# The last norm of a fused decoder layer, shared among three engines

## The chip, the cores and the metric

One Trainium2 chip, one core in use. The metric is the device time of one execution in microseconds (us). Engines: TensorE (PE in the profile), VectorE (DVE), ScalarE (ACT), GpSimd (POOL) and SyncE (SP), which here only starts DMA transfers. All data is float32; fp32r is the same 32 bits, written in the form that the matmuls read.

## The reference

One layer of a decoder on 544 tokens (512 of a prompt, 32 of 8 samples with 4 tokens each), 1024 channels. It has a joint input projection, dilated attention in three groups, a convolution branch, a merge with a norm, and then a mixture of 32 experts, of which each token uses two. What the change touches is the last step:

```python
def layer_norm(x, g, b):
    xf = x.astype(jnp.float32)
    mu = jnp.mean(xf, -1, keepdims=True)
    var = jnp.mean(jnp.square(xf - mu), -1, keepdims=True)
    return ((xf - mu) * lax.rsqrt(var + LN_EPS) * g.astype(jnp.float32) + b.astype(jnp.float32)).astype(x.dtype)

return layer_norm(DN_ALPHA * h + hierarchical_moe(h, ...), ln2_g, ln2_b)
```

`ln2_g` and `ln2_b` are vectors of 1024, one value for each channel.

## The kernel before, in words

The program is one launch with a written-out instruction list for each engine; semaphores order them. Its stages follow one another: projection (until about 165 us on GpSimd's side, with TensorE, ScalarE and VectorE), gates with attention and convolution (until about 420), merge of the two branches and first norm (L1424 to L1481), routing, and the 32 experts (from about 590 to 1143 us). There each weight matrix is split in two parts, the high one cast by ScalarE (L1153), the low one subtracted by VectorE (L1607), and multiplied on TensorE. GpSimd gathers the rows of an expert and scatters the results with an indirect DMA that adds in DRAM, into the buffer `expert_rows` (`y_dram`), which already holds the residual h. The experts' results come scaled by 1/alpha, so the buffer holds (alpha h + moe)/alpha, and the last norm uses EPS / ALPHA**2.

The tail begins when the last scatter has landed. GpSimd then raises `over_done` (L1823). SyncE, which waited for it (L524), loads the 544 rows in five tiles with five DMAs (L527), 128 rows of 1024 in each of the first four and 32 rows in the last (`TILES`, `NTT` = 5). The tiles `fh[0..3]` lie in `region_b`, `fh[4]` in `region_a`. `g2row` and `b2row` are `ln2_g` and `ln2_b`, broadcast to 128 partitions; they were loaded long before (L506, L507, semaphore `rows2_loaded`).

VectorE takes one tile after another (L1685 to L1692): `statistics` (L1441 to L1447: two `bn_stats` of 512 columns, `bn_aggr`, and an addition of eps) raises `hvar`; then it subtracts the mean and multiplies by `g2row` in one 1024-column `scalar_tensor_tensor` (L1689); waits for ScalarE's square root (L1245 to L1247, semaphore `hsd`); takes the reciprocal (L1691); and multiplies by it and adds `b2row` in a second 1024-column `scalar_tensor_tensor` (L1692), which raises `fdone`. The helper `link` makes VectorE wait for the completion of its own instruction before the next that reads its result. SyncE waits for `fdone` tile by tile and stores each tile to the output (L529 to L531). The small columns (`stats`, `mv`, `var_e`, `sd`, `rs`, `nmr`) exist twice and alternate from tile to tile.

ScalarE and GpSimd have nothing else to do in the tail: ScalarE takes the five roots, and after `over_done` GpSimd only waits for copies and stores that ended long before. Other lines that the rows name: L1294 is the convolution on VectorE (a `scalar_tensor_tensor` with two SBUF tensors, 128x512 and 128x32), L1710 GpSimd's part in splitting the projection's weights, L1739 GpSimd's sum of the two branches, beside which VectorE runs L1422 and L1435 (subtractions of SBUF tensors), L1428 and L1429 (one operand in PSUM). L1033, L1077 and L1082 are ScalarE's Identity of the gates, Sqrt and Silu of the convolution branch, and L1184 its scaling of an expert's result from PSUM.

Of the kernel before, what the change touches and what calls it, by code (L numbers as in the profile page):

```python
# [21 lines left out]
ACT = mybir.ActivationFunctionType  # L22
# [19 lines left out]
ALPHA = 2 ** 0.25  # L42
EPS = 1e-5
# [13 lines left out]
TILES = [(t * P, min(P, N - t * P)) for t in range((N + P - 1) // P)]  # L57
NTT = len(TILES)
# [51 lines left out]
def build(nc, a, o):  # L110
# [14 lines left out]
    with ExitStack() as ctx:  # L125
# [3 lines left out]
        def sem(name):  # L129
            return ctx.enter_context(nc.semaphore(name))  # L130
# [95 lines left out]
        def ln_cols(first, width=1):  # L226
            return [small[:, 18 * q + first:18 * q + first + width] for q in range(2)]

        stats, mv, var_e, sd, rs, nmr = ln_cols(0, 12), ln_cols(12, 2), ln_cols(14), ln_cols(15), ln_cols(16), ln_cols(17)
# [48 lines left out]
        def places(a_, b_):  # L278
# [56 lines left out]
        y_ps, y_used, hvar, hsd, hdone = (  # L335
            sem(x) for x in ("y_ps", "y_used", "hvar", "hsd", "hdone"))
# [14 lines left out]
        over_done = sem("over_done")  # L351
        fin_loaded = [sem(f"fin_loaded{t}") for t in range(NTT)]
        rows2_loaded = sem("rows2_loaded")
        fdone = sem("fdone")
        xg_zero, y_stored = sem("xg_zero"), sem("y_stored")
        qbd_zero, br_loaded = sem("qbd_zero"), sem("br_loaded")

# [2 lines left out]
        fh = [raw[0][:, t * D:(t + 1) * D] for t in range(4)] + [raw[2][:, 0:D]]  # L360
        g2row, b2row = raw[2][:, D:2 * D], raw[2][:, 2 * D:3 * D]
# [26 lines left out]
        def _(sp_e):  # L388
# [79 lines left out]
            for t in range(NTT):  # L468
                c0, n = TILES[t]
# [56 lines left out]
            for t, (c0, n) in enumerate(TILES):  # L526
                sp_e.dma_start(fh[t][0:n], y_dram[c0:c0 + n]).then_inc(fin_loaded[t], 16)  # L527
            for t, (c0, n) in enumerate(TILES):
                sp_e.wait_ge(fdone, t + 1)  # L529
                dst = y_p[:, t, :] if t < 4 else y_sample.rearrange("b t d -> (b t) d")  # L530
                sp_e.dma_start(dst, fh[t][0:n]).then_inc(y_stored, 16)  # L531
            sp_e.wait_ge(y_stored, 16 * NTT)
# [3 lines left out]
        def _(pe):  # L536
# [55 lines left out]
            def conv_rows(_):  # L592

                pe.wait_ge(u_set, 1)
                pe.wait_ge(state_sb, 1)
                for c in range(CT):
                    pe.transpose(ps[0:PAD, 6, c * P:(c + 1) * P], uext[:, c, SEQ:SEQ + PAD], eye)
                for c in range(CT):
                    last = pe.transpose(ps[0:NS, 7, c * P:(c + 1) * P], cst_u[:, c, :], eye)
                last.then_inc(u_ps, 1)  # L600
# [23 lines left out]
            def sample_rows(_):  # L624

                pe.wait_ge(v_sb, 6)
                for m in range(12):
                    last = pe.transpose(ps[0:NS, 2 + m // 4, (m % 4) * P:(m % 4) * P + P], zqkv[:, K0 + m, SEQ:N], eye)
                last.then_inc(s_ps, 1)
# [33 lines left out]
            def new_keys(_):  # L663
                pe.wait_ge(k_sb, 6)
                for m in range(6):
                    last = pe.matmul(ps[0:NS, 6, m * 64:(m + 1) * 64], zqkv[:, K0 + m, SEQ:N],
                                     qbd[:, m, :, :].rearrange("p b j -> p (b j)"), start=True, stop=True)
                last.then_inc(st_ps, 1)
# [315 lines left out]
        def _(ac):  # L984
# [251 lines left out]
            with ac.If(count > 0):  # L1236
                with ac.Fori(0, count) as i:
                    for f in range(KF):
# [3 lines left out]
                    ac.activation(yo[0].rearrange("p (h n) -> p h n", h=2), ps[0:BLK, 6:8, :], ACT.Identity,  # L1242
                                  scale=rowgate[:, bass.ds(i + NE, 1)]).then_inc(yo_sb, 1)

            for t, (c0, n) in enumerate(TILES):  # L1245
                ac.wait_ge(hvar, NTT + t + 1)
                ac.activation(sd[t % 2][0:n], var_e[t % 2][0:n], ACT.Sqrt).then_inc(hsd, 1)  # L1247


        @block.vector  # L1250
        def _(ve):
            chain = [0]

            def link(ins):

                chain[0] += 1
                ins.then_inc(dve_chain, 1)
                ve.wait_ge(dve_chain, chain[0])
# [165 lines left out]
            for m in range(KD):  # L1424
                s = 4 * (m % 2)
# [15 lines left out]
            def statistics(rows, s, n, done, eps):  # L1441

                for half in range(2):
                    st = ve.bn_stats(stats[s][0:n, 6 * half:6 * half + 6], rows[:, half * 512:(half + 1) * 512])
                link(st)
                link(ve.bn_aggr(mv[s][0:n], stats[s][0:n, :]))
                ve.tensor_scalar(var_e[s][0:n], mv[s][0:n, 1:2], eps, None, ALU.add).then_inc(done, 1)  # L1447
# [13 lines left out]
            for t, (c0, n) in enumerate(TILES):  # L1461
                s = t % 2
# [5 lines left out]
                hs = hrow[0:n, s, :]  # L1468
# [213 lines left out]


            ve.wait_ge(rows2_loaded, 32)
            for t, (c0, n) in enumerate(TILES):  # L1685
                s, hs = t % 2, fh[t][0:n]
                ve.wait_ge(fin_loaded[t], 16)
                statistics(hs, s, n, hvar, EPS / ALPHA ** 2)
                link(ve.scalar_tensor_tensor(hs, hs, mv[s][0:n, 0:1], g2row[0:n], ALU.subtract, ALU.mult))  # L1689
                ve.wait_ge(hsd, NTT + t + 1)  # L1690
                link(ve.reciprocal(rs[s][0:n], sd[s][0:n]))  # L1691
                ve.scalar_tensor_tensor(hs, hs, rs[s][0:n], b2row[0:n], ALU.mult, ALU.add).then_inc(fdone, 1)  # L1692


        @block.gpsimd
        def _(po):
# [118 lines left out]
            with po.If(count > 0):  # L1815
                with po.Fori(0, count) as i:
# [4 lines left out]
                    po.wait_ge(scattered[0], 16 * i + 16 * (NE // 2 + 1))  # L1821
                    po.sem_inc(pool_steps, 1)
            po.nop().then_inc(over_done, 1)  # L1823

            po.wait_ge(copied, 16 * 4 * NB)
            po.wait_ge(stored, 16 * STORES)
# [48 lines left out]
```

## Time and profile before

| | us |
|---|---|
| median of 3 runs (lowest to highest) | 1179.59 (1179.41 to 1184.06) |
| the profiled execution, its own time | 1181.13 |
| its span in the trace | 1179.10 |
| last norm, first statistics to end of span | 24.05 |

The span is what the trace covers; the execution's own time has 2.03 us more around it. Times in the trace count from the start of the span. PE is busy for 1102.8 us, DVE 820.6, ACT 582.3, POOL 268.2. A line of a group of instructions gives line, engine, operation, tile names, shapes, count, then busy time in all and the mean of one in ns, then idle time before them.

### The profile page before, as it was taken

To read this page: it belongs to the slowest core of one execution; us is meant where nothing else is said; L and a number is where in the kernel's file an instruction comes from. 1 tells how busy PE (TensorE), PEld (TensorE's weight loads), DVE (VectorE), ACT (ScalarE), POOL (GpSimd) and SP (SyncE) were. 2 spreads that over 40 slices of the span, in tenths; PEclk is the share of its full clock that TensorE was granted. 3 is DMA by queue.
4 is the path that set the end of the run, shared out by engine and by line. 5 is a ranking of instruction groups with operands and counts; after the bars stand their busy time and mean duration, and the time that the engine had idled before them with its cause. 6 is when DMAs were issued, how large, how long until landed. Compare 5 with 4: busy or idle time off the path is not lost.

```text
span 1179.1 us, 16033 instructions
## 1 busy us (share of the span) xinstructions
PE 1102.8 (94%) x5990; PEld 879.5 (75%) x5990; DVE 820.6 (70%) x929; ACT 582.3 (49%) x524; POOL 268.2 (23%) x185
## 2 busy tenths in 40 slices
PE   6999999999999999994999999999999999999970
PEld 5999998789888888763677777777777777777750
DVE  1079999810116728526699998888888888988857
ACT  2232221011115661003568777787787787787740
POOL 2344440000000015001022332322313313323100
PEclk9999999999999999986899999999999999999995
DMA  6476723136422540317699999999999999999813
GB/s 246 150 272 244 303 109 152 63 121 192 154 90 97 226 148 1 112 72 310 223 353 369 368 371 360 362 360 357 360 357 357 366 360 352 368 357 368 314 48 151
DMA packets 40336, 293.06 MB, mean 249 GB/s; under 512 B 10927, under 2 KB 14639, under 8 KB 24557
## 3 DMA queue, kind: packets, MB, share of 16 engines
q1 hardware_dynamic: 26029, 262.53, 58.9%
q0 software_dynamic: 10720, 25.98, 7.6%
q10 hardware_dynamic: 3552, 4.06, 1.0%
q8 instruction: 25, 0.41, 0.1%
q14 instruction: 10, 0.08, 0.0%
HBM read 286.83 MB, written 41.12 MB: 278 GB/s over the span
## 4 chain that ended last, share of the span: by engine, by line
PE 89%; DVE 4%; DMA 2%; POOL 2%; ACT 1%; issue 1%; POOLq 0%; SPq 0%; ACTq 0%; DVEq 0%
PE ps L587 10%; PE ps L902 10%; PE ps L904 10%; PE ps L903 10%; PE ps L926 5%; PE ps L928 5%; PE ps L927 5%; PE ps L549 3%; PE ps L551 3%; PE ps L550 3%; PE ps L805 3%; PE ps L885 2%; PE ps L770 2%; PE ps L659 2%; PE ps L833 2%; PE ps L835 2%
## 5 line engine op out<-in xcount | busy, mean ns | idle before, releaser
L1607 DVE TENSOR_TENSOR region_b_split<-region_b,z_split 128x2048 fp32r<-128x2048 f32 x96 | 216.9, 2286 | 26.0 <-ACT z_split L1153 25.5
L1607 DVE TENSOR_TENSOR region_a_split<-region_a,z_split 128x2048 fp32r<-128x2048 f32 x96 | 216.7, 2286 | 23.1 <-ACT z_split L1153 23.0
L902 PE MATMUL ps<-z_split,scratch_split 128*96 128x512 f32 x512 | 206.8, 404 | 1.9 <-DVE scratch_split L1612 1.9
L904 PE MATMUL ps<-z_split,scratch_split 128*96 128x512 f32 x512 | 202.1, 395 | 0.0
L1153 ACT CAST z_split<-region_a 128x2048 fp32r<-128x2048 f32 x96 | 179.8, 1908 | 0.0
L1153 ACT CAST z_split<-region_b 128x2048 fp32r<-128x2048 f32 x94 | 176.2, 1908 | 2.0 <-PE ps L904 2.0
L1294 DVE SCALAR_TENSOR_TENSOR z_conv_gates<-scratch,column_vectors,z_conv_gates 128x512 f32<-128x512 f32 (+1 forms) x240 | 133.9, 640 | 0.0
L587 PE MATMUL ps<-x_columns,region_b 128*128 128x272 f32 x512 | 127.1, 396 | 0.0
L549 PE MATMUL ps<-z_split,region_b_split 128*128 128x272 f32 x384 | 111.1, 289 | 3.5 <-POOL region_b_split L1710 3.5
L551 PE MATMUL ps<-z_split,region_b_split 128*128 128x272 f32 x384 | 111.2, 290 | 0.0
L904 PEld LDWEIGHTS ps<-z_split,scratch_split 128*96 128x96 f32 x512 | 83.2, 163 | 36.7
L902 PEld LDWEIGHTS ps<-z_split,scratch_split 128*96 128x96 f32 x512 | 85.3, 167 | 33.8 <-DVE scratch_split L1612 2.2
L550 PE MATMUL ps<-z_split,region_b_split 128*128 128x272 f32 x384 | 110.4, 288 | 0.0
L587 PEld LDWEIGHTS ps<-x_columns,region_b 128*128 128x128 f32 x512 | 94.4, 190 | 17.3
L926 PE MATMUL ps<-z_split,x_columns_split 128*96 128x512 f32 x256 | 101.1, 395 | 2.0 <-issue 1.2
L903 PE MATMUL ps<-region_b_split,scratch_split 128*96 128x512 f32 x256 | 101.5, 396 | 0.0
L928 PE MATMUL ps<-z_split,x_columns_split 128*96 128x512 f32 x256 | 100.9, 394 | 0.0
L903 PE MATMUL ps<-region_a_split,scratch_split 128*96 128x512 f32 x256 | 100.5, 393 | 0.0
L1710 POOL TENSOR_TENSOR region_b_split<-region_b,region_b_split 128x1024 fp32r<-128x1024 f32 x24 | 67.0, 2810 | 83.5 <-ACT region_b_split L1009 83.5
L1033 ACT ACTIVATE z_conv_gates<-ps,column_vectors 128x272 f32<-128x272 f32 x32 | 15.6, 487 | 124.7 <-PE ps L587 124.5
L549 PEld LDWEIGHTS ps<-z_split,region_b_split 128*128 128x128 f32 x384 | 72.3, 188 | 4.3 <-issue 3.0
L1771 POOL DMA_INDIRECT expert_rows<-value_rows,block_rows x26 | 67.6, 2600 | 23.2 <-POOL block_rows L1768 23.2
(262 smaller groups left out, 1757.4 us busy)
## 6 DMA issues: line engine op xcount, KB each, us to landing
region_b<-in_w_expert_gate SPq DMA_DIRECT2D x16, 2048.0 KB, 11.7
region_a<-in_w_expert_up SPq DMA_DIRECT2D x16, 2048.0 KB, 11.8
region_a<-in_w_expert_gate SPq DMA_DIRECT2D x16, 2048.0 KB, 11.7
region_a<-in_w_expert_down SPq DMA_DIRECT2D x16, 2048.0 KB, 11.4
region_b<-in_w_expert_up SPq DMA_DIRECT2D x16, 2048.0 KB, 12.2
region_b<-in_w_expert_down SPq DMA_DIRECT2D x16, 2048.0 KB, 11.4
region_b<-in_w_in_pairs SPq DMA_DIRECT2D x21, 1024.0 KB, 4.8
region_b<-in_cache_tiles POOLq DMA_DIRECT2D x16, 768.0 KB, 4.9
```

The source lines that it names most:

```text
L549: pe.matmul(out, w_hi[:, s, k, tile], x_hi[:, k, cols], start=k == 0, stop=False)
L550: pe.matmul(out, w_hi[:, s, k, tile], x_lo[:, k, cols], start=False, stop=False)
L551: last = pe.matmul(out, w_lo[:, s, k, tile], x_hi[:, k, cols], start=False, stop=k == KD - 1)
L587: last = pe.matmul(ps[:, half, 0:HALF], wring[:, j % 2, k, (t % 2) * P:(t % 2 + 1) * P], xt[:, k, half * HALF:(half + 1) * HALF], start=k ...
L902: pe.matmul(out, xh[:, k, :], hi[:, k, :], start=k == 0, stop=False)
L903: pe.matmul(out, xh[:, k, :], lo[:, k, :], start=False, stop=False)
L904: last = pe.matmul(out, xl[:, k, :], hi[:, k, :], start=False, stop=k == KD - 1)
L926: pe.matmul(out, hh[:, k, :], hi[:, k, cols], start=k == 0, stop=False)
L928: last = pe.matmul(out, hl[:, k, :], hi[:, k, cols], start=False, stop=k == KF - 1)
L1153: ac.copy(high_part[w][:, part], raw[place][:, part]).then_inc(high_set[w], 1)
L1294: ve.scalar_tensor_tensor(dst, win(k), wdw_c[:, bass.ds(k * CT + c, 1)], dst, ALU.mult, ALU.add).then_inc(conv_step, 1)
L1607: ve.tensor_tensor(low_part[place][:, part], raw[place][:, part], high_part[high or w][:, part].bitcast(F32), ALU.subtract).then_inc(low_s ...
```

## The change

For the four full tiles the norm is written as x * r + (-mean * r), then times `ln2_g`, then plus `ln2_b`, where r is the reciprocal root. ScalarE does the first (one `Identity` with scale and bias for each partition), VectorE the multiplication, GpSimd the addition. VectorE also computes -mean * r (`nmr`). VectorE takes the statistics of tile t+1 before the reciprocal of tile t, and multiplies tile t-1 after that. The fifth tile (32 rows) keeps the old form and comes last, with its statistics moved up.

```diff
@@ sync
             for t, (c0, n) in enumerate(TILES):
-                sp_e.wait_ge(fdone, t + 1)
+                if t < NTT - 1:
+                    sp_e.wait_ge(fdone, t + 1)
+                else:
+                    sp_e.wait_ge(fdone_last, 1)
@@ scalar
-            for t, (c0, n) in enumerate(TILES):
+            def last_root(t):
+                n = TILES[t][1]
                 ac.wait_ge(hvar, NTT + t + 1)
                 ac.activation(sd[t % 2][0:n], var_e[t % 2][0:n], ACT.Sqrt).then_inc(hsd, 1)
+
+
+            last_root(0)
+            for t in range(NTT - 1):
+                last_root(t + 1)
+                ac.wait_ge(frs, t + 1)
+                ac.activation(fh[t], fh[t], ACT.Identity, scale=rs[t % 2], bias=nmr[t % 2]).then_inc(fscaled, 1)
@@ vector
-            for t, (c0, n) in enumerate(TILES):
-                s, hs = t % 2, fh[t][0:n]
+            def last_statistics(t):
+                n = TILES[t][1]
                 ve.wait_ge(fin_loaded[t], 16)
-                statistics(hs, s, n, hvar, EPS / ALPHA ** 2)
-                link(ve.scalar_tensor_tensor(hs, hs, mv[s][0:n, 0:1], g2row[0:n], ALU.subtract, ALU.mult))
+                statistics(fh[t][0:n], t % 2, n, hvar, EPS / ALPHA ** 2)
+
+            def last_scale(t):
+                s = t % 2
                 ve.wait_ge(hsd, NTT + t + 1)
-                link(ve.reciprocal(rs[s][0:n], sd[s][0:n]))
-                ve.scalar_tensor_tensor(hs, hs, rs[s][0:n], b2row[0:n], ALU.mult, ALU.add).then_inc(fdone, 1)
+                link(ve.reciprocal(rs[s], sd[s]))
+                ve.scalar_tensor_tensor(nmr[s], mv[s][:, 0:1], -1.0, rs[s], ALU.mult, ALU.mult).then_inc(frs, 1)
+
+            def last_multiply(t):
+                ve.wait_ge(fscaled, t + 1)
+                ve.tensor_tensor(fh[t], fh[t], g2row, ALU.mult).then_inc(fmul, 1)
+
+            full = NTT - 1
+            last_statistics(0)
+            for t in range(full):
+                last_statistics(t + 1)
+                last_scale(t)
+                if t >= 1:
+                    last_multiply(t - 1)
+            last_multiply(full - 1)
+            t, n = full, TILES[full][1]
+            s, hs = t % 2, fh[t][0:n]
+            link(ve.scalar_tensor_tensor(hs, hs, mv[s][0:n, 0:1], g2row[0:n], ALU.subtract, ALU.mult))
+            ve.wait_ge(hsd, NTT + t + 1)
+            link(ve.reciprocal(rs[s][0:n], sd[s][0:n]))
+            ve.scalar_tensor_tensor(hs, hs, rs[s][0:n], b2row[0:n], ALU.mult, ALU.add).then_inc(fdone_last, 1)
@@ gpsimd, after over_done
+            po.wait_ge(rows2_loaded, 32)
+            for t in range(NTT - 1):
+                po.wait_ge(fmul, t + 1)
+                po.tensor_tensor(fh[t], fh[t], b2row, ALU.add).then_inc(fdone, 1)
```

## Rows read from the trace of the kernel before

**Rows 1.** The page: the chain that ended last, share of the span by engine.
```profile
PE 89%; DVE 4%; DMA 2%; POOL 2%; ACT 1%; issue 1%; POOLq 0%; SPq 0%; ACTq 0%; DVEq 0%
```

**Rows 2.** Busy time of each engine in the tail (x instructions), clock, DMA.
```profile
core 0: us, PE busy (x) PEld busy (x) DVE busy (x) ACT busy (x) POOL busy (x), PEclk, DMA share, GB/s
...
1155.05:1176.80 21.75, 0.00 (x0) 0.00 (x0) 21.02 (x35) 1.01 (x5) 0.00 (x0) 0.50 0.39 158
```

**Rows 3.** Timeline of tile 0 in the tail: start, duration, engine, line.
```profile
1155.05 1.28 DVE L1444 BATCH_NORM_STATS2 small<-region_b 128x6 f32<-128x512 f32 x2 [9.73 <-DMA region_b<-expert_rows]
...
1156.69 1.28 DVE L1689 SCALAR_TENSOR_TENSOR region_b<-region_b,small,region_a 128x1024 f32<-128x1024 f32 x1
1158.00 0.16 DVE L1691 RECIPROCAL small<-small 128x1 f32<-128x1 f32 x1
1158.20 1.28 DVE L1692 SCALAR_TENSOR_TENSOR region_b<-region_b,small,region_a 128x1024 f32<-128x1024 f32 x1
```

**Rows 4.** DMA issues of the tail: timeline, and median time to landing (last number).
```profile
1151.31 0.33 SPq L527 DMA_DIRECT2D region_b<-expert_rows  x1
...
region_b<-expert_rows SPq DMA_DIRECT2D x1, 512.0 KB, 3.6
...
1151.69 0.90 SPq L527 DMA_DIRECT2D region_b<-expert_rows  x2
...
region_b<-expert_rows SPq DMA_DIRECT2D x2, 512.0 KB, 4.1
...
1153.11 0.68 SPq L527 DMA_DIRECT2D region_a<-expert_rows  x1
...
region_a<-expert_rows SPq DMA_DIRECT2D x1, 128.0 KB, 6.4
...
out<-region_b SPq DMA_DIRECT2D x4, 512.0 KB, 2.6
out<-region_a SPq DMA_DIRECT2D x1, 128.0 KB, 1.9
```

**Rows 5.** Groups by form, with means; then L1710 and L1739, shortest/median/longest ns.
```profile
L1307 DVE TENSOR_TENSOR region_a<-region_a,value_rows 128x544 f32<-128x544 f32 x12 | 8.7, 725 | 0.4
...
L1607 DVE TENSOR_TENSOR region_b_split<-region_b,z_split 128x2048 fp32r<-128x2048 f32 x96 | 216.9, 2286 | 26.0 <-ACT z_split L1153 25.5 <-POOLq L1777 0.4
...
L1563 DVE SCALAR_TENSOR_TENSOR w_attn<-w_attn 128x10 f32<-128x10 f32 x4 | 0.7, 170 | 0.1
...
L1184 ACT ACTIVATE value_rows<-ps,row_gates 96x1024 f32<-96x1024 f32 x32 | 35.5, 1111 | 8.2 <-PE ps L928 8.2
...
L1710 POOL TENSOR_TENSOR region_b_split<-region_b,region_b_split x24: 2344/2393/4987, 16.5 to 164.2; 128x1024 fp32r<-128x1024 f32 x24
...
L1739 POOL TENSOR_TENSOR z_conv_gates<-z_conv_gates x8: 1344/2540/3317, 425.2 to 463.7; 128x544 f32<-128x544 f32 x8
```

**Rows 6.** Timeline of ScalarE around the Sqrt of the convolution branch.
```profile
355.59 0.61 ACT L1077 ACTIVATE ps<-ps 128x544 f32<-128x544 f32 x1
...
360.14 0.49 ACT L1033 ACTIVATE z_conv_gates<-ps,column_vectors 128x272 f32<-128x272 f32 x1 [3.94 <-PE ps L587]
360.64 1.28 ACT L1082 ACT_TABLE_LOAD   x1
```

**Rows 7.** Timelines of VectorE and GpSimd where they meet.
```profile
440.92 0.71 DVE L1429 TENSOR_TENSOR z_conv_gates<-ps,z_conv_gates 128x544 f32<-128x544 f32 x1
441.55 2.28 DVE L1435 TENSOR_TENSOR region_b_split<-region_b,region_a_split 128x2048 fp32r<-128x2048 f32 x1
443.75 1.86 DVE L1422 TENSOR_TENSOR z_split<-z_conv_gates,z_split 128x544 fp32r<-128x544 f32 x1
...
441.72 3.32 POOL L1739 TENSOR_TENSOR z_conv_gates<-z_conv_gates 128x544 f32<-128x544 f32 x1 [3.75 <-DVE z_conv_gates L1429]
...
86.24 2.42 DVE L1294 SCALAR_TENSOR_TENSOR z_conv_gates<-scratch,column_vectors,z_conv_gates 128x32 f32<-128x32 f32 x1
...
86.07 2.54 POOL L1710 TENSOR_TENSOR region_b_split<-region_b,region_b_split 128x1024 fp32r<-128x1024 f32 x1 [6.08 <-ACT region_b_split L1009]
```

More of the change, by code:

```diff
@@ L353, in build @@
         rows2_loaded = sem("rows2_loaded")
-        fdone = sem("fdone")
+        fdone, fdone_last, frs, fscaled, fmul = (sem(x) for x in ("fdone", "fdone_last", "frs", "fscaled", "fmul"))
         xg_zero, y_stored = sem("xg_zero"), sem("y_stored")
```

## The prediction, made before the changed kernel was built or timed

> **What bounds the kernel now.** I read the page first. The chain that ended last is 89% PE [rows 1], so over the whole kernel the matrix engine is the bound; the change touches only what comes after it, and the next view is the busy time by stretch from the moment the last norm begins. There PE, PEld and POOL have no work, DVE is busy 21.02 of the 21.75 us of the five tiles and ACT 1.01 [rows 2]. VectorE is therefore the bound of the tail: a fifth of that for each tile, a little over 4.3 us. The timeline of one tile [rows 3] gives the steps: 1.64 us from the first statistics instruction to the subtract-and-multiply (L1689), 1.28 for that, 0.16 for the reciprocal (0.20 to the next start), 1.28 for the multiply-and-add (L1692). These four follow each other without a gap, so ACT's square root (1.01 for five, 0.20 each [rows 2]) is hidden behind L1689. The loads of the tiles [rows 4] land at 1154.9 (1151.31 + 3.6) for tile 0 and at 1159.5 (1153.11 + 6.4) for tile 4; only the first is waited for. Tile 1, issued at 1151.69, takes about 4.6 (the mean of it and tile 0 is 4.1) and lands at 1156.3. The last store is issued at the end of the stretch of rows 2 and lands 1.9 later [rows 4]; the span, 1179.1, ends 0.4 after that. From the start of statistics of tile 0 (1155.05, which I call 0 from here) the end is thus at 24.05, made of 21.7 of VectorE and 2.3 of store and end.
>
> **The change, part by part.** Up to 0 nothing moves. In the four full tiles VectorE loses both 1024-column operations, 2 x 1.28, and gets one 1024-column tensor_tensor and one 128x1 scalar_tensor_tensor. Between 544 columns (725 ns) and 2048 columns (2286 ns) [rows 5] a tensor_tensor takes 1.04 ns a column, so 1024 columns take 725 + 480 x 1.04 = 1.22 us. The 128x1 one is near the 128x10 one, 0.17 us. A full tile costs VectorE 1.64 + 0.20 + 0.17 + 1.15 to 1.22, about 3.2 instead of 4.33. That saves 4.5 us of VectorE over four tiles, if nothing stops it.
>
> ScalarE gets a 1024-column Identity a tile. The nearest row is L1184, an Identity with a scale over 96x1024, 1.11 us [rows 5]; I take 1.10, and 1.3 would change nothing but the start of m3 below. With the root it is 1.3 us a tile, beside VectorE's 3.2, so it hides; if that cover went, only the one of tile 3 would be on the path, 1.1 us. Does Identity after Sqrt load a table? No: after the Sqrt of L1077 at 355.59, an Identity of L1033 ran at 360.14 with no load of its own; the next load (1.28) belongs to the Silu of L1082 [rows 6]. I cost table loads at nothing, and at 2 x 1.28 a tile if this were wrong.
>
> GpSimd gets four additions of 128x1024 f32. It did the same size and kind (a subtraction, L1710) in 2.34 at least and 2.39 in the median, and 128x544 in 1.34 at least [rows 5]. I take 2.39. But both rows have maxima, 4.99 and 3.32, and rows 7 show where they come from. At 441.72 GpSimd's 544-column addition meets VectorE's 2048-column subtraction (441.55, 2.28 long): it takes 3.32, so it ends 1.2 after VectorE's. VectorE's next, 544 columns, starts at 443.75 and takes 1.86 in place of 0.72: it ends 0.57 after GpSimd's. At 86.24 a VectorE scalar_tensor_tensor of only 32 columns takes 2.42, and ends 0.05 after GpSimd's 1024-column operation (86.07 + 2.54). So two operations that each read two SBUF tensors do not overlap at all; one waits the whole length of the other, and each turn under a wait gives back about 0.13 (3.32 - 2.11 = 1.21 against 1.34 own time; 0.57 against 0.72). In the new tail these are the addition, the multiply, the 128x1 scalar_tensor_tensor (two tensor inputs, however small) and both 1024-column operations of tile 4.
>
> The Trainium skill (SBUF — State Buffer, section "SBUF: two separate sides") calls this an exclusive lock and extends it to VectorE operations with one input where they run in a two-port mode. No row shows that beside a GpSimd addition; by it the 128x1 additions of the statistics would wait as well, the VectorE steps behind them would slip by about 0.35 in two tiles, and the sum would come to +1.5 instead of the value below.
>
> Now the order, with s statistics, r reciprocal, n the 128x1 operation, m multiply, a addition (times from 0):
> - s0 0, s1 1.64 (landed at 1.3), r0 3.28, n0 3.48, s2 3.65 (tiles 1 and 4 land at 1.3 and 4.5, tile 2 a third of the way, about 2.4), r1 5.29, n1 5.49, m0 5.66 to 6.88. ScalarE scaled tile 0 from 3.7 to 4.8, so m0 waits for nothing.
> - a0 6.97 to 9.36 (L1429 ends at 441.63 and the addition that waits for it starts at 441.72 [rows 7], so a hand-over is 0.09). Beside it s3 6.80 to 8.44 and r2; n2 at 8.64 is held until 9.4. m1 to 10.6.
> - a1 10.65 to 13.04, beside it s4 and r3; n3 at 12.35 is held to 13.07. m2 to 14.2.
> - ScalarE scales tile 3 only after n3, 13.13 to 14.23. m3 asks at 14.27, a2 at 14.29. From here on VectorE's two-input work and GpSimd's form one queue: m3 1.22, a2 2.39, first operation of tile 4 1.28, a3 2.39, second operation of tile 4 1.28.
> With a turn each: m3 to 15.5, a2 to 17.75, tile 4's first to 18.9, a3 to 21.1, tile 4's second to 22.3. Then 1.9 for the small store and 0.4 for the end: 24.6, which is 0.55 later than 24.05. Other turns are possible, since GpSimd's longest L1710 took 4.99 against 2.39 [rows 5], more than any single VectorE operation beside it there would make it wait, so it must have lost more than one turn. a2, a3, then tile 4: 25.0. Both of tile 4 ahead of a3: a3 ends at 22.3 to 22.5, its 512 KB store takes 2.6 [rows 4] and the small one follows it, 25.4. So +0.5 to +1.4; I take +0.8.
>
> Other edits cost nothing I can find: SP's extra semaphore only names the last wait; its order of stores is the same, and tile 4's is behind tile 3's, as above. GpSimd's additions stand behind over_done, which SP needs, but are only reached after it, and nothing behind them but the waits at the end of the program. Each store is issued later than now for tile 0 (9.4 in place of 4.4), and hides.
>
> The profiled execution was 1181.13 with a span of 1179.1; the median of the runs is 1179.59. The difference of +0.8 makes a span of 1179.9, and on the median 1180.4.
>
> **Rivals.**
> - *The two engines overlap after all.* Then a0 to 9.36, m1 8.8 to 10.0, a1 to 12.5, m2 to 13.2, a2 to 15.7, a3 to 18.05; VectorE is through at 16.9. Store of tile 3 to 20.7, of tile 4 to 21.1, end 21.5: -2.6, 1177.0. For it: these lines are not the same pair (additions in f32 and a multiply, where rows 7 have fp32r results and a subtraction). Against it: three pairs of shapes in two stages show whole waits.
> - *All of VectorE stands still under an addition, the statistics too.* This one ends slower. Then nothing overlaps after m0: VectorE's 5 x 1.64 + 4 x 0.37 + 4 x 1.2 + 2.7 = 17.2 and GpSimd's 9.56 give 26.8, less 0.8 for turns, and 2.3 for store and end: 28.3, +4.2, 1183.8. Place: s3, s4 and the reciprocals beside a0 and a1. It decides over my case as soon as a pair of batch_norm_stats (1.28 us [rows 3]) stretches beside an addition. Nothing shows a one-input operation beside one of GpSimd's additions; every wait that rows 7 show is of an operation with two tensor inputs, so I hold it unlikely. For a slowdown over 0.5% (5.9 us) each addition would have to be dearer than 2.39 by 0.4 us besides, or by 1.3 without this.
> - *Identity does reload the table*, so that ScalarE needs 3.9 a tile. It would be later than VectorE in tile 3 by up to 2.6: 1183.0. Rows 6 speak against it.
>
> **How the numbers follow.** The forecast (alternating turns) 0.82, overlap 0.07, all held 0.08, table loads 0.03. My case with its bounds is 1180.1 to 1181.0. The wider lock of the Trainium skill's SBUF page would give 1181.1. The runs before spread from 1179.41 to 1184.06 with two of three within 0.2. The range goes 2 below, towards overlap without reaching it, and 3 above to 1183.4, which takes in the table loads and an addition dearer by 0.5 each. A measurement of this kernel can tell about 0.5%, 5.9 us, from no change. Faster by that would need more than the whole saving of VectorE (4.5): 0.02. Slower by it needs the dearer additions just priced: 0.05. The rest, 0.93, is within it.
>
> **What would show it.** In the changed profile: POOL with four additions, 2.3 to 2.5 us where not waiting, longer late in the tail; multiplies of 1.2 us, at least one of 2 us or more; the 128x1 operation mean well over 0.17 us (two of four held by 0.7); a pair of batch_norm_stats still 1.28; one ACT table load in the tail; last store issued near 22.3 after the first statistics. I am wrong if the multiplies and additions lie beside each other at their own lengths, or if the statistics stretch.

## The result, and the profile after

The changed kernel takes 1189.11 us in the median of 14 runs (1183.97 to 1191.44); the kernel before, in the same number of runs, 1182.35 (1179.00 to 1186.38). The ratio is 1.0051, with a 95% interval of 1.0033 to 1.0068: slower by 6.0 us, with 3.9 and 8.0 as ends. A second measurement (below) gave 1.0044 (1.0021 to 1.0067). The forecast was +0.8 us with a range up to 1183.4; the kernel is slower than that.

The profiled execution of the changed kernel has a time of 1188.84 and a span of 1186.5. It splits at the first statistics of the last norm. Before, that was at 1155.05 with 24.05 behind it [rows 2]; now it is at 1158.14 with 28.36 behind it. So 3.1 us of the difference of these two executions lie ahead of anything that the change touches, and 4.3 in the tail. Another 0.3 lie outside the span: an execution's own time has 2.3 us more than its span here (2.0 before), and the same 0.3 shows in all 25 runs of the changed kernel against the 28 of the second measurement's kernel before; no run explains it. First the tail, in the timeline (start, duration, engine, line; idle time and releaser in brackets), from tile 2's statistics on:

```profile
1164.69 1.28 DVE L1455 BATCH_NORM_STATS2 small<-region_b 128x6 f32<-128x512 f32 x2
1164.93 2.34 POOL L1859 TENSOR_TENSOR region_b<-region_b,region_a 128x1024 f32<-128x1024 f32 x1 [15.39 <-DVE region_b L1709]
...
1166.51 0.77 DVE L1705 SCALAR_TENSOR_TENSOR small<-small 128x1 f32<-128x1 f32 x1
1167.20 1.21 DVE L1709 TENSOR_TENSOR region_b<-region_b,region_a 128x1024 f32<-128x1024 f32 x1
...
1172.06 2.34 POOL L1859 TENSOR_TENSOR region_b<-region_b,region_a 128x1024 f32<-128x1024 f32 x1 [1.23 <-DVE region_b L1709]
1172.15 3.33 DVE L1709 TENSOR_TENSOR region_b<-region_b,region_a 128x1024 f32<-128x1024 f32 x1 [0.17 <-ACT region_b L1258]
1175.40 1.27 DVE L1721 SCALAR_TENSOR_TENSOR region_a<-region_a,small 32x1024 f32<-32x1024 f32 x1
1175.56 3.31 POOL L1859 TENSOR_TENSOR region_b<-region_b,region_a 128x1024 f32<-128x1024 f32 x1 [1.16 <-DVE region_b L1709]
1176.70 0.15 DVE L1723 RECIPROCAL small<-small 32x1 f32<-32x1 f32 x1
1176.89 3.06 DVE L1724 SCALAR_TENSOR_TENSOR region_a<-region_a,small 32x1024 f32<-32x1024 f32 x1
...
1178.89 0.33 SPq L534 DMA_DIRECT2D out<-region_b  x1
1179.97 0.33 SPq L534 DMA_DIRECT2D out<-region_a  x1
```

These answer to [rows 3] and [rows 7]. VectorE and GpSimd take turns as forecast: the statistics (1.28, not stretched) lie beside an addition, while the 128x1 operation (0.77 instead of 0.16), the multiply of tile 3 (3.33 instead of 1.22) and the last operation (3.06 instead of 1.27) stand still under one. The last store starts at 1179.97, 21.83 after the first statistics. Before it was 21.74. Up to here the tail has lost 0.1 us.

But the span goes on to 1186.5. Before, 2.3 us followed the last store; now 6.5 do, and in them no engine is busy:

```profile
core 0: us, PE busy (x) PEld busy (x) DVE busy (x) ACT busy (x) POOL busy (x), PEclk, DMA share, GB/s
1158.14:1179.97 21.83, 0.00 (x0) 0.00 (x0) 21.08 (x35) 5.97 (x9) 10.32 (x4) 0.50 0.35 140
1179.97:1186.50 6.53, 0.00 (x0) 0.00 (x0) 0.00 (x0) 0.00 (x0) 0.00 (x0) 0.50 0.24 83
```

The instructions at the end of the program are not counted as busy and stand in no group. The view of one source line shows them: L125 is the `with` statement at whose exit each engine's list closes. Its columns are shortest/median/longest ns and the start. First the changed kernel, then the kernel before:

```profile
L125 PEldq DRAIN  x1: 752/752/752, 1147.3 to 1147.3; - x1
L125 ACTq DRAIN  x1: 1271/1271/1271, 1170.9 to 1170.9; - x1
...
L125 POOLq DRAIN  x1: 10503/10503/10503, 1175.8 to 1175.8; - x1
L125 DVEq DRAIN  x1: 3097/3097/3097, 1176.9 to 1176.9; - x1
...
L125 SPq DRAIN  x1: 13/13/13, 1182.2 to 1182.2; - x1
```

```profile
L125 POOLq DRAIN  x1: 7420/7420/7420, 1151.7 to 1151.7; - x1
...
L125 SPq DRAIN  x1: 13/13/13, 1178.9 to 1178.9; - x1
```

Each engine ends with a DRAIN, and then all of them meet. GpSimd's took 7.42 us before, from 1151.7 to 1159.1, while VectorE was at the end of the first tile, which it left at 1159.4: hidden by 19.8 us. Now it is issued at 1175.8, waits for the last addition (1175.56 + 3.31 = 1178.87), and ends at 1186.3, 7.43 after that. SyncE, which had seen all stores land at 1182.2, waited 4.1 us for GpSimd.

### The profile page after: what moved, and what is told of

It reads as the page before. It is cut to its first block, busy times and chain, and to the rows that moved or that the text cites. A ratio compares the mean times of both kernels' runs of the same rounds, so it can differ in the third digit from the quotient of the medians.

```text
span 1186.5 us, 16038 instructions
## 1 busy us (share of the span) xinstructions
PE 1106.3 (93%) x5990; PEld 883.6 (74%) x5990; DVE 820.6 (69%) x929; ACT 587.2 (49%) x528; POOL 278.6 (23%) x189
## 4 chain that ended last, share of the span: by engine, by line
PE 89%; DVE 4%; DMA 2%; POOL 2%; issue 1%; ACT 1%; POOLq 0%; SPq 0%; ACTq 0%; DVEq 0%
PE ps L590 10%; PE ps L905 10%; PE ps L907 10%; PE ps L906 10%; PE ps L929 5%; PE ps L931 5%; PE ps L930 5%; PE ps L552 3%; PE ps L554 3%; PE ps L553 3%; PE ps L808 2%; PE ps L888 2%; PE ps L773 2%; PE ps L662 2%; PE ps L836 2%; PE ps L837 2%
## 5 line engine op out<-in xcount | busy, mean ns | idle before, releaser
L590 PE MATMUL ps<-x_columns,region_b 128*128 128x272 f32 x512 | 130.5, 404 | 0.0
L1803 POOL DMA_INDIRECT expert_rows<-value_rows,block_rows x26 | 67.6, 2601 | 23.2 <-POOL block_rows L1800 23.2
```

Of the source, the lines that this page charges most:

```text
L590: last = pe.matmul(ps[:, half, 0:HALF], wring[:, j % 2, k, (t % 2) * P:(t % 2 + 1) * P], xt[:, k, half * HALF:(half + 1) * HALF], start=k ...
```

## The experiments

Nine of the twelve are single executions with a profile; three were also timed. I count the tail from the first statistics of the last norm to the end of the span, and give times in it from that point, as in the prediction. No matmul runs in it: two profiles of the changed kernel gave 28.36 and 28.45, and three kernels whose tail is that of before 24.05, 24.1 and 24.1, so one profile tells 0.1 us.

### Is it DRAIN, and what does it depend on?

The kernel before, with GpSimd made to wait for the last tile:

```diff
+            po.wait_ge(fdone, NTT)
             po.wait_ge(copied, 16 * 4 * NB)
```

> The kernel before with one wait more: at the end of its instruction list GpSimd waits for the last tile (fdone = 5) and does nothing in the tail. I count the tail from the first statistics of the last norm to the end of the span: 24.05 us before, 28.36 after the change. Theory A (GpSimd's DRAIN at the end of the program takes 7.4 us from GpSimd's last instruction, and the end of the program waits for it; it has nothing to do with the additions): the tail is 21.74 + 0.1 + 7.42 + 0.2 = 29.4 us, DRAIN stays 7.42. Theory C (the long end comes from the additions themselves): the tail stays at 24.1.

Measured: tail 29.5 us (1155.16 to 1184.7), DRAIN 7.42. A kernel with no addition on GpSimd loses 5.5 us by where its DRAIN lies. Theory C falls. DRAIN does not wait for a transfer of GpSimd either: it was issued at 1177.1, 22 us after the first tile of the tail, which is loaded only when the last scatter has landed, and it took the same 7.42.

With an early DRAIN besides:

```diff
             po.nop().then_inc(over_done, 1)
+            po.drain()
...
+            po.wait_ge(fdone, NTT)
```

> As the run before, with a DRAIN of GpSimd more, right behind over_done, that is over long before the end. Theory A (7.4 us whenever it runs): first and last DRAIN both 7.4, tail 29.4 us. Theory B (DRAIN works off what GpSimd's indirect DMAs of the experts have left, so the first one pays and a second is short, as the 0.18 us one at the start of the program): last DRAIN near 0.2, tail 24.1 us.

```profile
L1824 POOLq DRAIN  x1: 7420/7420/7420, 1156.8 to 1156.8; - x1
...
L125 POOLq DRAIN  x1: 40/40/40, 1182.4 to 1182.4; - x1
```

The early one (L1824) took 7.42 and the last one 0.04; the tail is 24.1 us. Theory A falls too: DRAIN has no fixed price, it works off something that an earlier DRAIN can work off.

The same line in the changed kernel:

> The changed kernel with a DRAIN of GpSimd right behind over_done, 10 us before its first addition. Theory A: tail 28.4 us as in the changed kernel. Theory B: last DRAIN short, the end is set by the last store, 21.83 + 2.1 + 0.4 = 24.3 us.

```profile
L1856 POOLq DRAIN  x1: 7420/7420/7420, 1157.0 to 1157.0; - x1
...
L125 POOLq DRAIN  x1: 3135/3135/3135, 1178.4 to 1178.4; - x1
```

Tail 24.7 us (1160.72 to 1185.4), in place of 28.4. The last DRAIN is issued beside the last addition and ends 0.1 us behind it, so additions add nothing to it. Theory B held, with a miss of 0.4: it gave 24.3. SyncE had seen the stores land at 24.1, as in the changed kernel, and the last 0.4 lie between two semaphore instructions of GpSimd (1184.9 and 1185.3); the same 0.4 is there in a second profile of this kernel, and no run explains it.

Three tiles shared, the addition of tile 3 on VectorE (SyncE's waits and GpSimd's loop, changed to match, are not shown):

```diff
-                ve.tensor_tensor(fh[t], fh[t], g2row, ALU.mult).then_inc(fmul, 1)
+                if t < 3:
+                    ve.tensor_tensor(fh[t], fh[t], g2row, ALU.mult).then_inc(fmul, 1)
+                else:
+                    link(ve.tensor_tensor(fh[t], fh[t], g2row, ALU.mult))
+                    ve.tensor_tensor(fh[t], fh[t], b2row, ALU.add).then_inc(fdone_v, 1)
```

> The changed kernel with the addition for tile 3 on VectorE (behind its multiply, 1.2 us) in place of GpSimd, which keeps tiles 0 to 2. Theory A: GpSimd's last addition ends near 16.3, DRAIN 7.45 later, tail 23.9 us; VectorE m3 to 17.3, addition to 18.4, tile 4 to 21.1, store and end 2.5: 23.6, so DRAIN still just decides. Theory C (additions on GpSimd are what costs): three of four are left, so tail 27 us or more.

Measured: tail 23.95 us (1153.25 to 1177.2). The multiply of tile 3 waited (3.33), everything after it ran at its own length, and DRAIN (9.52, issued at 14.2) ended at 23.7, just behind the stores at 23.4. One addition moved off GpSimd gains 4.4 us, because GpSimd's last addition ends 4.5 us earlier.

What does it work off? A DRAIN ahead of the expert stage, in the kernel before:

```diff
+            po.drain()
             po.wait_ge(idx_set, 1)
             po.wait_ge(h_stored[0], 96)
```

> The kernel before with a DRAIN of GpSimd just before its first gather of the expert stage, where it waits for the routing anyway; the DRAIN at the end stays where it is, hidden behind the tail, and its own duration is what counts. Theory B1 (what the last DRAIN works off was left by the indirect DMAs of the 32 experts): it stays 7.4 us. Theory B2 (it was left by GpSimd's work ahead of that: the plain DMAs of caches and rows, the splitting of weights): 0.04 us.

```profile
L1746 POOLq DRAIN  x1: 9359/9359/9359, 544.2 to 544.2; - x1
...
L125 POOLq DRAIN  x1: 5288/5288/5288, 1156.8 to 1156.8; - x1
```

Neither theory held: the last one takes 5.29 us. So something of the expert stage (64 indirect DMAs and no other heavy work of GpSimd) accounts for 5.3. It is not shown that the other 2.1 came from before it, for the DRAIN ahead of the experts took 9.36, more than the whole 7.42. GpSimd had issued its last two plain DMAs at 543.84 and 544.34, and the second took 8.2 us to land, at 552.5; the DRAIN ended 1.0 later, at 553.6. It may have waited for them, so its length is no price. At the start of the program, with no DMA of GpSimd behind it, its DRAIN takes 0.18 us. The three last DRAINs (7.42, 5.29, 0.04) fit a cost that grows with the DMAs GpSimd has issued since its last DRAIN, but the runs do not separate their number from their bytes or kind; what DRAIN works off stays open.

### Do the two engines exclude each other, and in which operations?

Without the additions (`ln2_b` left out in the four full tiles; the stores wait for `fmul`):

> The changed kernel without the additions of ln2_b in the four full tiles (they are left out; the stores wait for the multiply), so GpSimd does nothing in the tail and its DRAIN starts at once. Theory L (VectorE's operations with two SBUF inputs stand still while GpSimd adds): all multiplies 1.22 us, all 128x1 ones 0.16, VectorE through at 17.1 instead of 21.8, tail 17.1 + 2.5 = 19.6 us. Rival M (the stretched operations wait for something else, a store or ScalarE): they stay long and the tail is over 22 us.

```profile
1166.52 1.22 DVE L1709 TENSOR_TENSOR region_b<-region_b,region_a 128x1024 f32<-128x1024 f32 x1
...
1167.91 1.23 DVE L1709 TENSOR_TENSOR region_b<-region_b,region_a 128x1024 f32<-128x1024 f32 x1 [0.17 <-ACT region_b L1258]
1169.05 1.27 DVE L1721 SCALAR_TENSOR_TENSOR region_a<-region_a,small 32x1024 f32<-32x1024 f32 x1
1170.35 0.15 DVE L1723 RECIPROCAL small<-small 32x1 f32<-32x1 f32 x1
1170.54 1.27 DVE L1724 SCALAR_TENSOR_TENSOR region_a<-region_a,small 32x1024 f32<-32x1024 f32 x1
```

All at their own lengths, VectorE through at 16.7, tail 19.1 us. Against 21.8 with the additions, the exclusion costs VectorE 5.1 us, about all that the change had saved it (21.7 to 16.7). Theory L held.

Memsets instead of additions (`ln2_b` left out again; GpSimd writes and reads nothing), and then copies, which read one tensor (also without `ln2_b`):

```diff
-                po.tensor_tensor(fh[t], fh[t], b2row, ALU.add).then_inc(fdone, 1)
+                po.memset(raw[3][:, t * D:(t + 1) * D], 0.0).then_inc(fdone, 1)
```

> The changed kernel with a GpSimd memset of 1024 columns in a free place instead of each addition (ln2_b is not added in the four full tiles). GpSimd then writes and reads nothing, and keeps every semaphore. Theory R (only a GpSimd operation that reads SBUF blocks VectorE's two-input ones): memsets 0.95 us, multiplies 1.22, 128x1 ones 0.16, VectorE through at 17.1. Theory W (any GpSimd operation blocks): the 128x1 ones are not touched, as the memset is over before them, but the multiply of tile 3, which meets the memset of tile 2, takes 1.9 to 2.2 us. DRAIN still 7.4 us behind the last memset in both: the tail is about 14.6 + 0.95 + 7.6, 23.2 us or more.

> The changed kernel with a GpSimd copy of 1024 columns from SBUF to a free place in SBUF instead of each addition (one input; ln2_b is not added in the four full tiles). Theory R (a GpSimd operation that reads SBUF blocks VectorE's two-input ones, with one input as well as with two): a copy takes 1.0 to 1.3 us, and the multiply of tile 3 or what follows it, which meets a copy, takes 1.0 us more than its 1.22. Theory R2 (it takes two inputs on both sides): all stay at their own lengths, as with the memsets. DRAIN 7.4 us behind the last copy in both.

The multiply of tile 3 beside the memset, and beside the copy:

```profile
1168.31 0.95 POOL L1859 MEMSET region_a<- 128x1024 f32 x1 [2.04 <-DVE region_b L1709]
1168.42 1.23 DVE L1709 TENSOR_TENSOR region_b<-region_b,region_a 128x1024 f32<-128x1024 f32 x1 [0.17 <-ACT region_b L1258]
```

```profile
1166.08 1.04 POOL L1859 COPY region_a<-region_a 128x1024 f32<-128x1024 f32 x1 [1.96 <-DVE region_b L1709]
1166.19 2.00 DVE L1709 TENSOR_TENSOR region_b<-region_b,region_a 128x1024 f32<-128x1024 f32 x1 [0.17 <-ACT region_b L1258]
...
1168.26 2.03 POOL L1859 COPY region_a<-region_a 128x1024 f32<-128x1024 f32 x1 [1.14 <-DVE region_b L1709]
```

A memset leaves the multiply alone (1.23); a copy holds it until it is over (2.00), and is held in turn (2.03 against 1.04). So on GpSimd's side one SBUF input is enough, and writing alone does nothing. Theory R. The tails were 22.7 and 24.6 us, each ended by a DRAIN 7.4 behind GpSimd's last operation; for the memsets 23.2 or more had been expected, and VectorE was ahead of that plan by 0.5 us (last memset at 14.1 in place of 14.6).

The 128x1 operation with one tensor input:

```diff
-                ve.scalar_tensor_tensor(nmr[s], mv[s][:, 0:1], -1.0, rs[s], ALU.mult, ALU.mult).then_inc(frs, 1)
+                ve.tensor_scalar(nmr[s], mv[s][:, 0:1], -1.0, rs[s], ALU.mult, ALU.mult).then_inc(frs, 1)
```

> The changed kernel with -mean * r as a tensor_scalar (one tensor input, the reciprocal as a scalar for each partition) instead of a scalar_tensor_tensor of two tensor inputs. Theory L1 (only operations with two SBUF tensors wait): all four take 0.15 us instead of 0.16, 0.16, 0.77, 0.73, ScalarE scales tiles 2 and 3 earlier by 0.6, the wait moves to the multiplies of tiles 1 and 2 (1.8 us each), and the last one of tile 3 still waits: tail within 0.3 of 28.4 us. Theory L2 (the small one-input operations wait as well): they stay near 0.75 in tiles 2 and 3 and nothing else changes.

```profile
1167.19 2.34 POOL L1859 TENSOR_TENSOR region_b<-region_b,region_a 128x1024 f32<-128x1024 f32 x1 [15.44 <-DVE region_b L1709]
1168.27 0.21 DVE L1457 BATCH_NORM_AGGREGATE small<-small 128x2 f32<-128x12 f32 x1
1168.51 0.15 DVE L1458 TENSOR_SCALAR small<-small 128x1 f32<-128x1 f32 x1
1168.58 0.15 DVE L1704 RECIPROCAL small<-small 128x1 f32<-128x1 f32 x1
...
1168.77 0.21 DVE L1705 TENSOR_SCALAR small<-small 128x1 f32<-128x1 f32 x1
1168.90 1.71 DVE L1709 TENSOR_TENSOR region_b<-region_b,region_a 128x1024 f32<-128x1024 f32 x1
```

Under the addition (until 1169.53) all of VectorE's one-input operations run at their own lengths; the new form takes 0.21, and the wait moves to the multiply (1.71, and 1.67 for tile 2). L1 held, with one miss: the multiply of tile 3 took its turn ahead of the addition (1.21), and tile 4's first operation had the wait (3.35). The tail is 28.1 us, as it must be while DRAIN ends it.

### The time, and the 3.1 us ahead of the tail

The changed kernel again, and the one with the early DRAIN, timed:

> The changed kernel once more, beside the kernel before on one chip. The tail in the profile is 28.3 to 28.4 us again (it holds no matmul, so the clock cannot touch it). If the tail's 4.3 us are all that the change costs, the ratio of the times is 1.0036 and the moment at which the tail begins is spread alike in both kernels, in steps of half the length of the stretches at half clock; if the change costs something ahead of the tail as well, it is 1.005 as in the first measurement.

> The changed kernel with the early DRAIN, timed. Its tail was 24.66 us, 0.6 over that of before and 3.7 under that of the change. If nothing ahead of the tail costs anything, the ratio to the kernel before is 1.0005 and the difference cannot be told.

Measured: 1.0044 (1.0021 to 1.0067) and 1.0006 (0.9986 to 1.0025). 4.3 us of 1180 are 1.0036, and 0.6 are 1.0005: both intervals hold the value that the tail alone gives, but the first also holds 1.005, so by itself it does not rule out a further cost. The tail of the repeated change is 28.45 us, and it began at 1153.35, not at 1158.14. The ends of the two samples say more than the ratio: the shortest run of the change is 4.5 us above the shortest of the kernel before, and the longest 4.7 above the longest, close to the tail's 4.3 and the 0.3 outside the span. In the first measurement they were 5.0 and 5.1 apart. The times lie on several levels, and what the first ratio has above that is probably which of them the 14 runs of either kernel hit; no run shows it. Where do such shifts come from? The busy time by stretch, first of the changed kernel's first profile, then of the kernel before, in the stage of the gates:

```profile
300.00:315.00 15.00, 15.00 (x80) 12.43 (x79) 2.58 (x8) 3.53 (x6) 0.00 (x0) 1.00 0.39 126
315.00:326.00 11.00, 11.00 (x43) 8.53 (x42) 0.00 (x0) 0.97 (x2) 0.53 (x1) 0.69 0.56 197
326.00:341.00 15.00, 15.00 (x91) 13.24 (x89) 3.85 (x9) 1.12 (x3) 0.53 (x1) 1.00 0.18 59
```

```profile
315.00:326.00 11.00, 11.00 (x63) 9.40 (x63) 0.00 (x0) 0.97 (x2) 0.53 (x1) 1.00 0.62 210
```

The granted clock falls from 1.00 (2.4 GHz) to 0.69 on the mean of 11 us, part of it at 1.2 GHz, although TensorE was busy all the time before and in it; 43 matmuls are done instead of 63. 0.31 x 11 = 3.4 us are lost, about the 3.1 by which this profile's tail began later. Such dips come and go: in the stretch 165:420 the mean clock was 1.00 in three profiles (the kernel before, the change repeated, the last version below) and 0.97 to 0.99 in three others (the change, and both kinds with an early DRAIN). The tail began between 1153.2 and 1155.6 in eight of the 14 profiles and between 1158.1 and 1160.7 in the other six; kernels whose tail is that of before are in both groups, and so are the two profiles of the change. No run connects them with the change. They go with the levels of the times: of the 28 runs of the kernel before, the five shortest (1178.9 to 1179.4) have a mean granted clock of 0.972, the six longest (1185.8 to 1186.2) of 0.966, and 0.006 of 1180 us is 7.1.

### A version from these findings

```diff
@@ scalar
-            last_root(0)
             for t in range(NTT - 1):
-                last_root(t + 1)
+                last_root(t)
                 ac.wait_ge(frs, t + 1)
                 ac.activation(fh[t], fh[t], ACT.Identity, scale=rs[t % 2], bias=nmr[t % 2]).then_inc(fscaled, 1)
+            last_root(NTT - 1)
@@ vector
             for t in range(full):
-                last_statistics(t + 1)
                 last_scale(t)
-                if t >= 1:
-                    last_multiply(t - 1)
-            last_multiply(full - 1)
+                last_statistics(t + 1)
+                last_multiply(t)
```

together with the early DRAIN, the one-input form of -mean * r, and additions on GpSimd for tiles 0 to 2.

> A version from what the runs showed: a DRAIN of GpSimd right behind over_done; additions on GpSimd for tiles 0 to 2 only, on VectorE for tile 3; -mean * r with one tensor input; and the reciprocal of a tile ahead of the statistics of the next, so that each addition lies beside a reciprocal, -mean * r and statistics, none of which reads two SBUF tensors. By hand: m0 3.9 to 5.1, additions 5.2 to 7.5, 8.7 to 11.0, 12.2 to 14.5, VectorE through at 19.4, tail 21.9 us, with the last DRAIN short. That is 2.2 us under the kernel before (24.05), 0.2% of 1180, so the timed runs should not tell the two apart. If reordering brings nothing, the tail is that of the run with three shared tiles, 23.9.

```profile
1160.12 0.15 DVE L1706 RECIPROCAL small<-small 128x1 f32<-128x1 f32 x1
1160.31 0.21 DVE L1707 TENSOR_SCALAR small<-small 128x1 f32<-128x1 f32 x1
1160.36 2.35 POOL L1864 TENSOR_TENSOR region_b<-region_b,region_a 128x1024 f32<-128x1024 f32 x1 [14.10 <-DVE region_b L1712]
1160.44 1.28 DVE L1457 BATCH_NORM_STATS2 small<-region_b 128x6 f32<-128x512 f32 x2
...
1162.07 1.72 DVE L1712 TENSOR_TENSOR region_b<-region_b,region_a 128x1024 f32<-128x1024 f32 x1
...
1174.77 0.33 SPq L536 DMA_DIRECT2D out<-region_a  x1
```

Each addition now lies beside one-input work, and only 0.5 us of each is waited for. The last store starts at 19.7 (21.7 before), and the tail is 22.05 us (1155.05 to 1177.1): 2.0 less than before, 6.3 less than the change. Timed, the ratio to the kernel before is 0.9988 (0.9970 to 1.0007), where the tail would give 0.9983: better than the change, and not to be told from the kernel before by its time. No run separates the new order from the one-input form; together they took VectorE from 21.3 (three tiles shared, old order) to 19.7.

## Why the prediction was wrong

**The step that failed** is the sentence that GpSimd's additions have "nothing behind them but the waits at the end of the program", priced at nothing. Behind them was GpSimd's DRAIN, 7.42 us, whose cover was the whole tail. The additions moved GpSimd's last work from before the tail to 20.7 in it, and the term that was missing is max(0, 20.73 + 7.43 + 0.2 - 24.3) = 4.1 us, where 24.3 is the end that the stores alone would set (21.83 + 2.1 to landing + 0.4). The profile of before had it in the view of L125; I read only the views that count busy time and named waits. The step asked what was queued behind the additions, and stopped at the last line of the written program instead of the last instruction of the engine.

**What held.** The exclusion between the engines was read rightly from [rows 7] and cost what was said: m1 to m3, both operations of tile 4 and the 128x1 ones. VectorE was through at 21.8 against 22.3 forecast. The difference is not the order of turns. I had m3 ask at 14.27 and a2 at 14.29, close to a tie, and a2 came first by 0.09 (13.92 to 14.01), but the same five operations stand in the queue either way. It began 0.35 us earlier (13.92) and was 0.15 shorter. I had charged VectorE 0.17 for each 128x1 operation, its whole duration, and the next instruction starts 0.08 after it:

```profile
1163.48 0.16 DVE L1705 SCALAR_TENSOR_TENSOR small<-small 128x1 f32<-128x1 f32 x1
1163.56 1.22 DVE L1709 TENSOR_TENSOR region_b<-region_b,region_a 128x1024 f32<-128x1024 f32 x1
```

Durations: addition 2.34 (2.39), multiply 1.22 (1.22), 128x1 0.16 (0.17). ScalarE's scaling took 1.24 where I took 1.10 from [rows 5]; its source is SBUF here and PSUM there. It stayed hidden except for 0.17 us ahead of m3. No table was loaded between root and Identity, as said; the one load that the list of signs put in the tail lies ahead of it, at 1149.77. The two held 128x1 operations waited 0.6 us each, where 0.7 was said.

**The rivals.** Overlap: no. All of VectorE held: no, the statistics and the small one-input operations ran freely under additions. By the wider rule of the Trainium skill (SBUF — State Buffer, section "SBUF: two separate sides"), as the prediction applied it, the 128x1 additions of the statistics would have waited. They took 0.15 us beside an addition, so they do not; whether they run in the two-port mode of which the page speaks, no run shows. None of the rivals had its mechanism at the end of the program, and that is where the 4 us went. That the rival of all VectorE held came to +4.2, next to the 4.3 measured in the tail, is chance.

**The level.** The forecast stood on a median of three runs, 1179.59. Fourteen and 28 runs of the same kernel gave 1182.35 and 1182.51, because the dips in the clock make several levels between 1178.9 and 1186.4 and two of my three runs had the lowest. A center of +0.8 was thus 2.8 us low before the change came in. With both corrected, and the 0.3 outside the span, 1182.35 + 4.3 + 0.3 = 1187.0, inside what the interval of the ratio allows (1186.3 to 1190.4). The chance of 0.05 for slower by over 0.5% was too small; the two ratios, 1.0051 and 1.0044, lie on either side of that line.

## What to carry to other kernels

Before giving an idle engine work near the end, look at what closes its instruction list: here a hidden DRAIN of GpSimd, 7.4 us long, became the end of the program, and an explicit one placed in idle time took nearly all of it away. Moving additions from VectorE to GpSimd paid here only for the part that lay beside VectorE operations with at most one SBUF tensor input; order the work so that additions meet statistics, not multiplies. A median of three executions is no level where the clock dips in some executions and not in others; read the change in a stretch that holds no matmul.

## What was not expected of the hardware

GpSimd's DRAIN took 7.42 us after the kernel's DMAs, 5.29 when one DRAIN had been run ahead of the expert stage, 0.04 when one had been run just before, and 0.18 at the start of the program. A GpSimd memset of 1024 columns (0.95 us) did not hold a VectorE multiply (1.23), a copy (1.04) did (2.00). TensorE's clock went down for some microseconds in the middle of dense matmuls (0.69 on the mean of 11 us) in some executions and not in others of the same kernel; what starts it was not tried.
